# Giving out PSUM banks inside the order planner, pinning the opening's loads, more planning passes, and norm products on GpSimd

## The reference

```
h    = modulate(rms_norm(x))                      # scale and shift from silu(c) @ mod_w
proj = h @ w_in     -> q (16 heads), k, v (4 heads), pool channels (512), gate logits (2 x 1024)
q, k = rope(rms_norm per head)                    # axial rotary tables
a    = attention over +-128 tokens and 256 context keys, with a sink   -> @ w_attn_proj
p    = centred means over 2/4/8/16 tokens minus the token itself       -> @ w_pool_proj
x    = x + g1 * ((sigmoid(ga) * a + sigmoid(gp) * p) @ w_out)
x    = x + g2 * swiglu(modulate(rms_norm(x)))     # w_up, w_down, d_ff 2816
```

## Time and profile before

| | us |
|---|---|
| median of 3 runs | 1055.45 (1054.94 to 1177.26) |
| the profiled execution | 1056.16 |
| its span on core 0, the slowest | 1054.6 |
| busy in the span: PE | 989.3 (94%) |
| DVE, ACT, POOL | 514.4, 476.7, 211.7 |

### The profile page before, as it was taken

One profiled execution on the slowest core, in us unless ns is written; L12 is line 12 of the kernel. 1 busy time (PEld: TensorE's weight loads), 2 busy tenths in 40 slices (PEclk: granted clock), 3 DMA queues, 4 the chain that ended last, 5 costly groups with the idle time before them and its releaser, 6 DMA issues.

```text
span 1054.6 us, 15129 instructions; the slowest of 8 cores (1046.4 to 1054.6 us)
## 1 busy us (share of the span) xinstructions
PE 989.3 (94%) x6206; PEld 465.1 (44%) x6206; DVE 514.4 (49%) x925; ACT 476.7 (45%) x639; POOL 211.7 (20%) x239
## 2 busy tenths in 40 slices
PE   1577897999999999999999999999999999999998
PEld 0334453544444444455444444444444444444443
DVE  3489977776656656553247642124322135321244
ACT  2478876687988788663228841110011100111100
POOL 0231433655334547211210000000000000000000
PEclk9689988999999999999999999999999999999999
DMA  9986746733444547903760034220042220022034
GB/s 233 297 244 149 121 74 108 124 57 58 75 63 60 89 62 110 171 1 69 260 170 1 1 72 78 40 41 0 10 83 39 40 40 1 3 38 41 1 145 174
DMA packets 24502, 90.80 MB, mean 86 GB/s; under 512 B 2672, under 2 KB 3568, under 8 KB 20976
## 3 DMA queue, kind: packets, MB, share of 16 engines
q0 software_dynamic: 16416, 53.71, 30.9%
q1 hardware_dynamic: 8016, 36.11, 9.7%
HBM read 135.14 MB, written 8.39 MB: 136 GB/s over the span
## 4 chain that ended last, share of the span: by engine, by line
PE 86%; DMA 6%; DVE 5%; ACT 2%; issue 1%; POOL 0%; SPq 0%; DVEq 0%; POOLq 0%
PE psall L1320 29%; PE psall L1046 18%; PE psall L1334 14%; PE psall L1249 5%; PE psall L650 5%; PE psall L838 4%; PE psall L884 4%; PE psall L941 3%; DMA m1f<-mod 2%; DMA xstc<-ctxT 2%; DVE pT L856 1%; DMA m2w<-mod 1%; PE psall L779 1%; PE psall L898 1%; ACT pT L851 1%
## 5 line engine op out<-in xcount | busy, mean ns | idle before, releaser
L1320 PE MATMUL psall<-h2T,wu 128*128 128x512 bf16 x1408 | 304.7, 379 | 0.0
L1320 PEld LDWEIGHTS psall<-h2T,wu 128*128 128x128 bf16 x1408 | 137.8, 98 | 166.1
L1323 ACT ACTIVATE sil<-psall 128x512 f32<-128x512 f32 x88 | 52.5, 597 | 338.6 <-PE psall L1320 338.5
L1324 DVE TENSOR_TENSOR actT<-psall,sil 128x512 bf16<-128x512 f32 x88 | 60.9, 692 | 234.3 <-PE psall L1320 228.4
L851 ACT ACTIVATE pT<-psall 128x1024 bf16<-128x1024 f32 x160 | 158.0, 1023 | 18.8 <-PE psall L838 17.8
L1334 PE MATMUL psall<-actT,wd 128*128 128x512 bf16 x704 | 152.4, 379 | 0.0
L1337 DVE SCALAR_TENSOR_TENSOR xacc<-psall,dotc,xacc 128x512 f32<-128x512 f32 x96 | 72.1, 751 | 80.1 <-PE psall L1334 80.1
L1334 PEld LDWEIGHTS psall<-actT,wd 128*128 128x128 bf16 x704 | 68.9, 98 | 83.0
L1046 PE MATMUL psall<-hall,rg 128*128 128x512 bf16 x320 | 75.6, 379 | 0.6 <-ACT csc L1068 0.6
L425 POOL DMA_DIRECT2D wu<-w_up_p x22 | 11.8, 534 | 282.6 <-PE psall L1320 280.4
L856 DVE TENSOR_TENSOR pT<-pT,cmt 128x1024 bf16<-128x1024 bf16 x64 | 59.6, 932 | 15.8 <-ACT pT L851 15.6
(11 more groups left out here) (186 smaller groups left out, 1274.7 us busy)
## 6 DMA issues: line engine op xcount, KB each, us to landing
rg<-w_c POOLq DMA_DIRECT2D x60, 256.0 KB, 4.0
wu<-w_up_p POOLq DMA_DIRECT2D x22, 512.0 KB, 5.0
m1f<-mod SPq DMA_DIRECT2D x8, 1024.0 KB, 30.0
m2w<-mod POOLq DMA_DIRECT2D x16, 512.0 KB, 7.0
xacc<-xT SPq DMA_DIRECT2D x4, 2048.0 KB, 8.6
out<-xacc SPq DMA_DIRECT2D x32, 256.0 KB, 2.1
cw<-w_c POOLq DMA_DIRECT2D x6, 768.0 KB, 19.8
xsta<-xT SPq DMA_DIRECT2D x2, 2048.0 KB, 12.1
```

Source lines behind the costliest of these rows:

```text
L1320: T.op("pe", lambda e, k=k, ab=ab: e.matmul(ps[bs + ab], lhsT=wu[us][:, ab, k, :], rhs=h2T[:, k, cc * 512:(cc + 1) * 512], start=(k == 0), ...
L1323: T.op("act", lambda e: e.activation(out=sil[si][:], in_=ps[bs], func=AF.Silu), reads=[PS(bs)], writes=[slk], tab="si")
L1324: T.op("dve", lambda e: e.tensor_tensor(out=actT[:, fi, cc * 512:(cc + 1) * 512], in0=ps[bs + 1], in1=sil[si][:], op=ALU.mult), reads=[PS( ...
```

## The change

- `fbank`, the product with V and the transposes no longer get a fixed bank: `T.bank()` returns a nameless `Bank`, and `forward` gives it one of the banks 4 to 7 when it plans the first operation that uses it (the latest freed that is free by then, else the one that is free first). The end of a bank's use is planned too, and `backward` sees the links of the last plan. Addresses are looked up at replay (`Banks`, `late=True`, lambdas). As rotation no longer orders them, a few dependencies are written out (`tailop`, `transop`, `lastop`).
- From `T.lead = True` to `False`, the groups recorded are put in `first`: in every pass but the initial one they come before all others, in program order. These are the loads fcon, ropf, xsta, m1f0 to m1f7, cmt, wkv, the small operations behind them, and `make_rope(0)`, which is moved up there; `make_rope(1)` follows right behind.
- PASSES goes from 12 to 40.
- `chunk_norm` gives the eight L522 products of chunks 2 and 3 to POOL in place of DVE.

```diff
-PASSES = 12
+PASSES = 40
+    def share_banks(self, banks):
+        for b in banks:
+            st = self.state[("ps", b)]
+            self.pool0.append((b, ([st["w"]] if st["w"] is not None else []) + list(st["r"])))
+    def bank(self):
+        v = Bank(len(self.vbanks))
+        self.vbanks.append(v)
+        return v
...
+            if g in self.vneed:
+                fit = [x for x in spare if x[0] <= t + 1e-9]
+                it = max(fit) if fit else min(spare)
+                spare.remove(it)
+                held[self.vneed[g]] = it[1]
+                extra.append((g, it[1], it[2]))
...
-            cur = self.forward(preds, succ, [-x for x in tail], TABWAIT)
+            cur = self.forward(preds, succ, [g - 1e6 if g in self.first else -x for g, x in enumerate(tail)], TABWAIT)
...
+    T.lead = True
     dma("sp", fcon[:], fcond, ("fcon",), "fcon")
     dma("sp", ropf[:], ropefd, ("ropf",), "ropf")
     load_x(0, "a")
...
+    make_rope(0)
+    T.lead = False
+    make_rope(1)
...
-        return Norm(s, CH[ci][1], 0, lambda k: hT[ci][:, k, :], lambda k: ("hT%d" % ci, k), ssb, False)
+        return Norm(s, CH[ci][1], 0, lambda k: hT[ci][:, k, :], lambda k: ("hT%d" % ci, k), ssb, ci in (2, 3))
...
     def fbank():
-        bank["fb"] += 1
-        return bank["lo"] + bank["fb"] % (8 - bank["lo"])
+        return T.bank()
...
+    T.share_banks((4, 5, 6, 7))
...
-            ob = 4
+            ob = T.bank()
...
+    T.end_share()
```

More of the change, by code:

```diff
@@ L45, in __init__, with __getitem__ @@
         self.sb = False
+class Bank:
+    __slots__ = ("n", "ops", "idx")
+    def __init__(self, idx):
+        self.n, self.ops, self.idx = None, [], idx
+class Banks:
+    def __init__(self, aps):
+        self.aps = aps
+    def __getitem__(self, i):
+        return self.aps[i.n if isinstance(i, Bank) else i]
 class Trk:
@@ L66, in __init__ @@
         self.bias = 0
+        self.first = set()
+        self.vbanks = []
+        self.pool0 = []
+        self.lead = False
     def tile(self, off, shape, dtype, name):
@@ L130, in op @@
             self.prio.append(g + self.bias)
+            if self.lead:
+                self.first.add(g)
         self.groups[g].append(o)
@@ L146, in forward @@
         free = {e: 0.0 for e in self.ENG}
+        done_t = [0.0] * ng
+        uses = [len(x) for x in self.vusers]
+        held = {}
+        spare = []
+        wait0 = []
+        for b, gs in self.pool0g:
+            wait0.append([b, gs, len(gs)])
+            if not gs:
+                spare.append((0.0, b, None))
+        extra = []
         wire = 0.0
@@ L175, in forward @@
             for e in self.ENG:
-                if not ready[e]:
+                cand = ready[e] if spare else [g for g in ready[e] if g not in self.vneed]
+                if not cand:
                     continue
-                now = [g for g in ready[e] if late(g, e) <= free[e]]
+                now = [g for g in cand if late(g, e) <= free[e]]
                 if now:
@@ L188, in forward @@
                     best = (key, e, g, t, c)
+            if best is None:
+                return None
             _k, e, g, t, c = best
@@ L209, in forward, with backward @@
                         ready[e2].append(h)
-        return end, order, start, used, took
-    def backward(self, preds, succ, start, used, took):
+        return end, order, start, used, took, extra
+    def backward(self, preds, succ, start, used, took, extra):
         ng = len(self.groups)
+        preds = [set(x) for x in preds]
+        for g, b, v in extra:
+            preds[g].update(self.vusers[v] if v is not None else self.pool0d[b])
+        succ = [[] for _ in range(ng)]
+        for g in range(ng):
+            preds[g].discard(g)
+            for h in preds[g]:
+                succ[h].append(g)
         left = [len(x) for x in succ]
@@ L418, in build_program @@
     psall = nc.alloc_psum_tensor("psall", [128, 4096], F32)
-    ps = [psall[:, i * 512:(i + 1) * 512] for i in range(8)]
+    ps = Banks([psall[:, i * 512:(i + 1) * 512] for i in range(8)])
     def PS(i):
```

104 lines of the change are left out of this document (74 added, 30 removed).

## The result

| | us | |
|---|---|---|
| before, median of 5 | 1055.45 | |
| changed, median of 5 | 1060.21 | ratio 1.0047, 95% interval 1.0031 to 1.0063 |

The change makes the kernel 5 us slower, where 13.5 us faster was forecast. 1060.21 lies just outside the range of 1028 to 1060, and on the wrong side of 1055.

A forecast was written before the change was run, and what follows sets the result against it. PE bounds the kernel, with 23.3 us idle and 13.1 us of lost clock at 55 to 200 us. Terms -3.0 - 4.5 - 2.5 - 3.5 = -13.5 against 1056.2 give 1042.7, forecast 1042 as median; range 1028 to 1060.

The forecast's parts named there:

- the term for the norm products: Norms of chunks 2 and 3: sixteen products moved to POOL take some 12 us off DVE; -2.5 us.
- two cases at 120 us: DVE and POOL products overlapping at 120 us in the trace; each time the later one lost about 1.0 us.
- Rival (b): Shared-port lock: each of sixteen products costs or suffers 1.0 us, +4 net, no clock back; about 1052, chance 0.18.
- rival (d): Slower: GpSimd bounds both norms, products of 2.26 us, PE starves behind the modulations; 1077, chance 0.07.
- Banks: PE's waits for a PSUM bank, half of 9.0 us saved; -4.5 us (-9.0 to 0).
- the prediction's four: PE's bank waits: L884 on Otok 4.1, L628 2.6, L1105 1.3, L632 on dotc 1.0; 9.0 us.
- Opening: Before 55 us: tables made early bring chunk 0's last modulation 3.5 us sooner, less 0.5 for issues; -3.0 us.
- wq0 and xsta would cancel: Opening loads: wq0 issued 3.4 us later, xsta started 3.5 us sooner; together nothing, +3.4 if they do not cancel.
- Clock: 55 to 200 us: seven us less PE idle regains clock at 0.56 us per us; -3.5 us (-8 to 0).
- Forty passes: Planner passes: no added instruction, worth already claimed by the other terms; 0, within 3 us either way.
- (c): Planner's best of forty by its own costs may be no better on the chip; 1056, +-3, chance 0.12.

The follow-up runs named there:

- x1: Changed kernel, plan frozen, the sixteen norm products of chunks 2 and 3 on DVE in place of POOL; ratio 0.9963 to the kernel before.
- z1: Kernel before with only the norm products of chunks 2 and 3 moved to POOL, newly planned; ratio 1.0093 to the kernel before.
- y1: All of the change but the products on POOL (they stay on DVE), newly planned; ratio 1.0085 to the kernel before.
- y4: All of the change but the banks, which are handed out in turn as before, newly planned; ratio 1.0047 to the kernel before.
- u3: Change without the pinned opening, that plan frozen, then norm products and pooling sums on DVE; ratio 0.9986 to the kernel before.
- x6: Changed kernel, plan frozen, norm products and pooling sums on DVE; ratio 0.9947 to the kernel before.
- x2: Changed kernel, plan frozen, wq0 issued behind block 5 in place of block 6; ratio 1.0026 to the kernel before.
- x3: Changed kernel, plan frozen, norm products on DVE and wq0 issued behind block 5; ratio 0.9964 to the kernel before.
- u4: Changed kernel, plan frozen, norm products and pooling sums on DVE and wq0 issued behind block 5; ratio 0.9960 to the kernel before.
- y2: All of the change but the pinned opening, newly planned, products on POOL; ratio 1.0175 to the kernel before.
- m1: Separate program timing eight DVE instructions of a kind alone, then beside eight POOL products; SBUF-only kinds 3.74 to 9.61 and 4.91 to 10.81 us, PSUM readers unchanged.

## Why the prediction was wrong

**The step that failed is the term for the norm products, -2.5.** It measured +8.9 in the frozen plan (x1) and +9.8 alone on the kernel before (z1, newly planned). Newly planned without it, the change is 4 us slower still (y1), which the plans' scatter covers. The forecast counted work taken off the fullest engine, 12 us, and priced a collision at 1.0 us, from two cases at 120 us. What it missed is that a DVE instruction on SBUF may wait for a row of POOL instructions, and that this stops all of DVE, PSUM readers included: two modulations were held 6.32 and 4.52 us, and PE waited 5.58 and 2.66 us behind them. Rival (b) named the right mechanism and 1052, rival (d) the right side and place. (d) had POOL as the slow engine, products of 2.26 us each, where POOL ran them at 1.26 and DVE paid. The evidence was in the trace of before and was not looked for: of its 64 masks the median is 0.69 us and the longest 3.81:

```profile
L856 DVE TENSOR_TENSOR pT<-pT,cmt x64: 661/693/3808, 91.2 to 480.8; 128x1024 bf16<-128x1024 bf16 x64
```

**Banks, -4.5:** nothing as planned (y4 against the changed kernel). The 11 us between the two plans with DVE free are not shown to be theirs. The waits did not go: the prediction's four came to 9.0 us, and in the changed kernel PE waits for readers of banks under other names, 5.6, 5.1, 2.9, 1.6 and 1.5 us. The prediction had warned of a late reader on DVE; the longest of these stand behind instructions that POOL's rows held, not behind DVE's load.

**Opening, -3.0:** right at its own place, 3.5 us at the last modulation; 4 us in the pair u3 and x6, which are two plans. That wq0 and xsta would cancel was wrong at xsth, 5.2 us late on the slowest core; at the end wq0's place is worth 2 us or nothing (x2, x3, u4).

**Clock, -3.5:** the wrong sign. It was tied to idle time, 0.56 us per us. On the slowest cores idle time fell by 3.3 us and the mean granted clock rose from 0.976 to 0.981 (over all eight it is 0.981 and 0.980), yet PE took 7.4 us longer for the same matmuls, 4.2 by the medians. A mean over the span counts idle time: on the slowest core of before the clock was 0.78 in the opening, where PE was busy 20.9 of 55 us, and on that of the changed kernel it was 1.00 there and 0.74 at 80 to 100 us, with 18.2 us of work. Other cores have it elsewhere; two have 1.00 at 80 to 100. Why it was granted where it was is not shown. The nearest case with a cause is 348.23: a wait of 3.70 us, then matmuls at half speed.

**Forty passes, 0 within 3:** 2 us better than twelve, not separable from the scatter of newly planned kernels.

**Range.** It ended at 1060, where no row stood but (c)'s +-3; rival (d)'s weight of 0.07 was too small for a mechanism that the trace showed twice in two overlaps.

## What to carry to other kernels

Before work is moved to GpSimd, list for VectorE every instruction that reads SBUF alone, with the longest of its kind beside the median. A longest of several times the median, beside a row of GpSimd instructions, is a stall of the whole engine, and it is worth what waits behind it, not what it does. A planner that lacks this rule can find plans that are shorter on paper and place rows of one engine before critical work of the other. Keep one side of each pair off the shared path: here modulations to ScalarE and sums on VectorE gave 0.9930 with the order left as it was. Compare busy time for an unchanged number of matmuls over all cores, not the mean clock. Judge parts of a planned kernel with the plan frozen as well as newly planned: here taking the same part out came to -9 us frozen and +4 us newly planned, so a difference of 10 us between two plans says little of the part.

## What the runs showed of the hardware

- A VectorE instruction was passed over by up to nine GpSimd instructions in a row (10.64 us in y2, 11.17 in z1, where it had begun by its record at 126.92, 0.26 us before the first of eight). It alternated with them in m1 (none over 1.53 us), where both engines had a full queue of such instructions, and in the kernel before, beside seven products of the rotary tables in a row from 46.23 us (none over 1.53 us either).
- What decides between the two is open. The rows that held VectorE had products of two different tensors in them (1.26 us a product), those of m1 read one tensor twice (1.04); and before four of the five long instructions told of here VectorE had one on PSUM, before the fifth (160.43) a reciprocal in SBUF. Neither was varied.
- One of the stalled instructions is a tensor_scalar with a single SBUF tensor, f32 to bf16 (6.32 us at 111.21; 3.74 to 9.61 us for eight in m1). An instruction that reads PSUM beside SBUF is free of it (4.88 us alone and beside).
- A GpSimd-issued load in the middle of the row did not let VectorE in at 114.14 to 114.75 us, nor at 161.55. Behind the last product of a row it did: in y2 the mask ends at 130.17, inside the load issued at 129.57, and in the kernel before the longest mask at 420.72, inside the one issued at 420.11.
